# Two-layer diffusion trunk on one core: order of branch A's score matmuls, and two small PE jobs each placed one step later

## What is computed

```python
qa = qa.reshape(B, T, A_KV_HEADS, A_GROUP, HD)          # 2 key heads, 4 query heads each
s = jnp.einsum("bqhgd,bshd->bhgqs", qi, k) * scale
m = jnp.maximum(jnp.max(s, axis=-1, keepdims=True), sink)
e = jnp.exp(s - m)
p = e / (jnp.sum(e, axis=-1, keepdims=True) + jnp.exp(sink - m))
o = jnp.einsum("bhgqs,bshe->bqhge", p, v)
merged = ga * (oa @ w_branch_a) + gb * (od @ w_branch_b) + gc * (om @ w_branch_c)
```

## Time and profile before

| what | value |
|---|---|
| median of 3 runs | 1704.36 us (1704.34 to 1705.16) |
| the profiled execution, its own time | 1704.68 us |
| span from its first to its last instruction | 1702.9 us |
| mean granted TensorE clock, share of full speed | 0.997 |
| instructions in the trace | 21,074 |
| busy: PE, DVE, ACT, POOL | 98%, 25%, 19%, 7% of the span |
| moved by DMA | 561.94 MB, mean 330 GB/s |

### The profile page before, as it was taken

The page is one execution under the profiler, slowest core; times in us unless marked ns, Lnnn a source line. Parts: engine busy times, 40 slices in busy tenths (PEclk is TensorE's granted clock), DMA queues, the critical chain, the costliest instruction groups (busy, mean ns, idle before and its releaser), DMA issues. The chain is left out here.

```text
span 1702.9 us, 21074 instructions
## 1 busy us (share of the span) xinstructions
PE 1665.1 (98%) x8107; PEld 892.7 (52%) x8107; DVE 430.7 (25%) x1183; ACT 324.8 (19%) x786; POOL 120.0 (7%) x164
## 2 busy tenths in 40 slices
PE   5999999999999999999999999999999999999998
PEld 3778788543333333333368878884433333333332
DVE  1114444361111111111131444543411111111112
ACT  1010341121111111111120113403111111111111
POOL 3001000020000000001020000001100000000000
PEclk9999999999999999999999999999999999999999
DMA  9994233379999999999999732235899999999993
GB/s 388 397 410 164 76 117 118 118 282 419 425 426 424 425 425 426 425 425 424 420 389 422 292 115 99 99 110 207 323 426 425 426 425 425 426 425 424 426 425 159
DMA packets 61100, 561.94 MB, mean 330 GB/s; under 512 B 13020, under 2 KB 13168, under 8 KB 21072
## 3 DMA queue, kind: packets, MB, share of 16 engines
q1 hardware_dynamic: 45504, 529.55, 75.4%
q0 software_dynamic: 15504, 31.09, 5.3%
HBM read 575.95 MB, written 6.88 MB: 342 GB/s over the span
## 5 line engine op out<-in xcount | busy, mean ns | idle before, releaser
L1050 PE MATMUL PS<-ring,region 128*64 128x512 f32 x2048 | 451.0, 592 | 0.7 <-ACT region L1331 0.7
L1050 PEld LDWEIGHTS PS<-ring,region 128*64 128x64 f32 x2048 | 146.4, 137 | 290.4 <-issue 290.3
L617 PE MATMUL PS<-region,ring 128*128 128x256 f32 x1088 | 245.3, 381 | 0.5 <-DMA ring<-in_blocks 0.5
L1099 PE MATMUL PS<-region 128*128 128x512 f32 x512 | 241.0, 594 | 0.0
L1076 PE MATMUL PS<-ring,region 128*64 128x512 f32 x1024 | 233.8, 598 | 0.2
L617 PEld LDWEIGHTS PS<-region,ring 128*128 128x128 f32 x1088 | 203.8, 190 | 34.2 <-issue 6.3
L1804 DVE SCALAR_TENSOR_TENSOR region<-region,PS 128x256 f32<-128x256 f32 x64 | 26.9, 421 | 662.8 <-ACT region L1338 662.8
L510 PEld LDWEIGHTS PS<-const,region 128*128 128x128 f32 (+1 forms) x925 | 106.5, 141 | 115.7 <-issue 67.3
L510 PE MATMUL PS<-const,region 128*128 128x128 f32 (+1 forms) x925 | 137.8, 278 | 15.7 <-DMA region<-in_c 9.6
L1076 PEld LDWEIGHTS PS<-ring,region 128*64 128x64 f32 x1024 | 67.7, 136 | 157.4 <-issue 156.7
L1344 ACT ACTIVATE region<-PS 128x512 f32<-128x512 f32 x128 | 76.4, 597 | 265.9 <-PE PS L1076 265.9
(11 more groups left out here) (270 smaller groups left out, 991.2 us busy)
## 6 DMA issues: line engine op xcount, KB each, us to landing
ring<-in_expert_blocks SPq DMA_DIRECT2D x192, 2048.0 KB, 17.1
ring<-in_blocks SPq DMA_DIRECT2D x120, 1024.0 KB, 19.6
region<-post_rows POOLq DMA_DIRECT2D x8, 512.0 KB, 6.2
h_first<-region POOLq DMA_DIRECT2D x4, 512.0 KB, 6.4
h_table<-region POOLq DMA_DIRECT2D x4, 512.0 KB
region<-in_w_kvk POOLq DMA_DIRECT2D x2, 640.0 KB, 18.6
region<-in_mla_w_ukv POOLq DMA_DIRECT2D x2, 512.0 KB, 21.8
region<-in_post_pack POOLq DMA_DIRECT2D x2, 512.0 KB, 25.4
```

What stands on the lines that cost most here:

```text
L617: last = pe.matmul(PS[:, j % 2, m * T:(m + 1) * T], w[:, k, m * P:(m + 1) * P], hT[:, k, :], start=(k == 0), stop=(k == KC - 1))
L1050: last = pe.matmul(PS[e * CAP:(e + 1) * CAP, 0, :], xe[:, k, e * CAP:(e + 1) * CAP], w[:, k % 4, :], start=(k == 0), stop=(k == KC - 1), s ...
L1099: last = pe.matmul(PS[:, 4 + 2 * t + half, :], hot[:, t * P:(t + 1) * P], og[:, half * HALF:(half + 1) * HALF], start=False, stop=True, sk ...
```

## The change

Three edits, of which the second and third don't touch branch A.

- Scores of branch A: a unit now takes the same slots of both key heads in turn, each key head into a bank of its own (b and b + 1), so the heads of a unit are others than before: tile 0's unit g has slots 2g and 2g + 1 of both key heads, tile 1's unit g has slot g of both. The values, the place of the weight blocks, the exponentials' sources, the row maxima and the sink terms follow. The outputs stand in `qA` by slot, and the rows of `w_branch_a` are put in that order on the host. As two banks are written, the scores of units 0 and 1 wait for one more emptied job each.
- Counts: they come behind step 5 of the shared gate/up of tile 1 instead of behind step 4.
- List transposes: they come ahead of k = 3 of pair 0's gate/up instead of ahead of k = 2.

```diff
--- before.py
+++ after.py
@@ -779,16 +779,16 @@
                     q0, k0, kn = t * P, t * P, P + t * P
                     if u < 2:
 
-                        pe.wait_ge(prep_ev, l * PREP_JOBS + (21, 23)[u])
+                        pe.wait_ge(prep_ev, l * PREP_JOBS + (22, 24)[u])
                     else:
 
                         pe.wait_ge(prob_exp, (l * UNITS + u - 1) * 4)
                     n = 4 if t == 0 else 2
                     for i in range(n):
                         if br == "A":
-                            h = n * g + i
-                            kv, c = h // 4, h % 4
-                            last = pe.matmul(PS[:, b, i * kn:(i + 1) * kn], qA[HD * kv:HD * (kv + 1), c, q0:q0 + P],
+                            j, kv = divmod(i, 2)
+                            c = (n // 2) * g + j
+                            last = pe.matmul(PS[:, b + kv, j * kn:(j + 1) * kn], qA[HD * kv:HD * (kv + 1), c, q0:q0 + P],
                                              kA[HD * kv:HD * (kv + 1), k0:k0 + kn], start=True, stop=True)
                         elif br == "B":
 
@@ -825,7 +825,7 @@
                             h = heads * g + i
                             tile = kt + t
                             if br == "A":
-                                v = vA[:, tile, (h // 4) * HD:(h // 4 + 1) * HD]
+                                v = vA[:, tile, (i % 2) * HD:(i % 2 + 1) * HD]
                             elif br == "B":
                                 v = vB[:, tile, h * P:(h + 1) * P]
                             else:
@@ -834,7 +834,7 @@
                                 out = PS[:, 7, i * P:(i + 1) * P]
                             else:
                                 out = PS[HD * (i % 2):HD * (i % 2) + HD, 7, (i // 2) * P:(i // 2 + 1) * P]
-                            blk = i * (t + 1) + kt
+                            blk = (i % 2 * (heads // 2) + i // 2 if br == "A" else i) * (t + 1) + kt
                             weights = probT[:, u % 2, blk * P:(blk + 1) * P]
                             if br == "B":
                                 last = pe.matmul(out, weights, v, start=(kt == 0), stop=(kt == t), skip_group_check=True)
@@ -983,7 +983,7 @@
                 logits(1)
                 for half in range(2):
                     token_rows(1, half)
-                shared_gate_up(1, range(5))
+                shared_gate_up(1, range(6))
 
                 pe.wait_ge(sel_ready, l + 1)
                 pe.matmul(PS[:, 0, 0:N_EXPERTS], ones, sel[:, 0, :], start=True, stop=False)
@@ -995,7 +995,7 @@
                 for t in range(2):
                     last = transpose(PS[0:N_EXPERTS, 1, P + t * P:P + (t + 1) * P], sel[:, t, :])
                 last.then_inc(keys_tr, 1)
-                shared_gate_up(1, range(5, KC))
+                shared_gate_up(1, range(6, KC))
 
                 def first_tokens():
                     for t in range(2):
@@ -1044,7 +1044,7 @@
                                 n = 6 * g + 2 * (k // 4) + e
                                 if k % 4 == 0 and e == 0:
                                     arrived_pair(n, base)
-                                if g == 0 and k == 2 and e == 0:
+                                if g == 0 and k == 3 and e == 0:
                                     transpose_lists()
                                 w = ring[:, n % RING_SLOTS, :].rearrange("p (k c) -> p k c", k=4)
                                 last = pe.matmul(PS[e * CAP:(e + 1) * CAP, 0, :], xe[:, k, e * CAP:(e + 1) * CAP], w[:, k % 4, :],
@@ -1232,7 +1232,7 @@
                         act.activation(sinke[:, u % 2, 0:n], sinke[:, u % 2, 0:n], ACT.Exp).then_inc(sink_exp, 1)
                     for i in range(n):
                         m, j = divmod(i, n // 2)
-                        src = PS[:, b + m, j * kn:(j + 1) * kn] if br == "B" else PS[:, b, i * kn:(i + 1) * kn]
+                        src = PS[:, b + m, j * kn:(j + 1) * kn] if br in "AB" else PS[:, b, i * kn:(i + 1) * kn]
                         act.activation(prob[:, u % 2, i * kn:(i + 1) * kn], src, ACT.Exp,
                                        scale=(C_QK if br == "C" else HD) ** -0.5, bias=negm[:, u % 2, i:i + 1],
                                        accum_out=psums[:, u % 2, i:i + 1]).then_inc(prob_exp, 4 // n)
@@ -1606,16 +1606,17 @@
                     n, kn = (4, P) if t == 0 else (2, 2 * P)
                     scale = (C_QK if br == "C" else HD) ** -0.5
                     m = negm[:, u % 2, 0:n]
-                    if br == "B":
+                    if br in "AB":
                         s = PS[:, b:b + 2, 0:(n // 2) * kn].rearrange("p m (j k) -> p m j k", k=kn)
                         step(ve.reduce_max(m.rearrange("p (m j) -> p m j", m=2), s, X))
                     else:
                         step(ve.reduce_max(m, PS[:, b, :].rearrange("p (i k) -> p i k", k=kn), X))
                     if br == "A":
 
-                        ns = nsink[:, n * g:n * g + n]
+                        ns = nsink[:].rearrange("p (m c) -> p m c", m=2)[:, :, (n // 2) * g:(n // 2) * (g + 1)]
+                        m, e = (v.rearrange("p (m j) -> p m j", m=2) for v in (m, sinke[:, u % 2, 0:n]))
                         step(ve.scalar_tensor_tensor(out=m, in0=m, scalar=-scale, in1=ns, op0=ALU.mult, op1=ALU.min))
-                        ve.tensor_tensor(sinke[:, u % 2, 0:n], m, ns, ALU.subtract).then_inc(negm_ready, 1)
+                        ve.tensor_tensor(e, m, ns, ALU.subtract).then_inc(negm_ready, 1)
                     else:
                         ve.tensor_scalar(m, m, -scale, None, ALU.mult).then_inc(negm_ready, 1)
 
@@ -1874,9 +1875,10 @@
         put(L_UQ, w["mla_w_uq"][l])
         for j in range(10):
             put(L_GL + j, w_in[:, GL + 256 * (j + 2):GL + 256 * (j + 3)])
+        by_slots = w["w_branch_a"][l].reshape(A_KV, A_HEADS // A_KV, HD, -1).swapaxes(0, 1).reshape(A_HEADS * HD, -1)
         for half in range(2):
-            for b, name in enumerate(("w_branch_a", "w_branch_b", "w_branch_c")):
-                put(L_BR + 3 * half + b, w[name][l][:, 512 * half:512 * half + 512])
+            for b, matrix in enumerate((by_slots, w["w_branch_b"][l], w["w_branch_c"][l])):
+                put(L_BR + 3 * half + b, matrix[:, 512 * half:512 * half + 512])
         gate_up = np.concatenate([w["shared_w_gate"][l], w["shared_w_up"][l]], axis=1)
         for rows in range(2):
             for half in range(2):
```

## The result

The changed kernel takes **1712.31 us** (median, 1711.53 to 1713.75) against 1704.36 (1704.03 to 1705.16) for the kernel before: a ratio of 1.0043, with a 95% interval of 1.0032 to 1.0055. The median is higher by 8.0 us, clear of the noise, where no change was forecast, and it lies above the range. The profiled execution took 1713.43 us with a span of 1711.6 (before 1704.68 and 1702.9), so the two spans can be set beside each other: + 8.7 us.

The account below looks back on a forecast made before the run. The prediction took TensorE, busy for 98% of the span, as the bound. It summed - 5.1 us (scores) and + 4.6 us (later gather) to - 0.5 us, so 1703.9 us in the median's terms, no change, range 1697.6 to 1707.8.

Parts of the forecast that it names:

- Part 1: Branch A's scores: heads alternating halves and banks run at branch B's times, 5.1 us saved over both layers.
- The cover of 1.05 us: Branch A's unit step: 1.05 us spare between DVE's normalising and the weight transposes, so no new wait.
- Part 2: Counts one step later: wait before L989 gone, 0.45 us gained per layer, the rest a new wait before L1002.
- Part 3: List transposes one step later: L1032's wait gone, but pair 1's gather lands later, + 2.0 and + 2.6 us by layer.
- The line: Pair 1's gather time interpolated between leads of 1.32 and 0.01 us over the ring's load: 7.3 and 7.7 us.
- the 0.44 us of the prediction: Expected time from issue of pair 1's gather to issue of the ring's 2 MB load, 1.32 - 0.88 us.
- pair 2's gather: Gather issued 0.01 us ahead of the load, 8.7 and 9.2 us; used as the short-lead end of the interpolation.
- some 4 us: Expected PE wait on the table's rows for pair 1, in place of 0.6 and 0.85 us.
- Behind the load: Rival: pair 1's gather lands only with the ring's load, at 384.2 and 1220.5; 1707.8 us, chance 0.08.
- the rule of the Trainium skill: DMA engines take queues in turn, draining whole packets; read as the gather standing behind the load's share, not between its pieces.
- The gather isn't disturbed: Rival: pair 1's gather, still issued first, keeps its 4.32 and 4.56 us; - 6.6 us, 1697.8, chance 0.22.
- no overlap in part 1: Rival: branch A's halves don't overlap in the scores, so the 5.1 us falls away; 1709 us, chance 0.03.

Follow-up runs that it names:

- the run with the filled wait: Changed kernel plus seven unused 128x128 by 512 matmuls on PE between pair 0's gate/up and the wait for the gather; 1707.86 us, ratio 1.0018.
- a lead of 0.90: Kernel before plus sixteen tiny POOL memsets ahead of pair 1's gather, so the ring's load follows it by 0.90 and 0.93 us; 1709.46 us, ratio 1.0025.

## Why the prediction was wrong

**Part 1** held: 5.6 and 2.9 us by form and - 5.1 us measured alone. The cover of 1.05 us before the transposes was enough in branch A: the list of waits has 0.5 us on L1636 in two places, and the kernel before has the same 0.5 on L1635.

**Part 2** held by its own steps: L989 without a wait, a new wait before L1002 (0.25 us a layer where 0.4 was expected), and 0.6 us measured with an interval that can't confirm the size.

**Part 3** held as far as PE's waits go (none on L1032, none on L1813 behind the gathered rows). The prediction failed at one step of it: "Between leads of 1.32 and 0.01 us I go in a straight line". The line gave 7.3 and 7.7 us; measured were 9.9 and 10.0. That is 2.6 and 2.3 us too little even though the lead came out kinder than the 0.44 us of the prediction. The lead was 0.73, because DVE was free when the transposes came: from L1032 to POOL's issue took 372.07 - 370.44 = 1.63 us and not the 375.22 - 373.32 = 1.90 of the earlier trace rows. At 0.73 the line would have given 6.3. The table above shows no such line: the gather takes 3.9 to 5.3 us down to a lead of 1.2, 5.7 at 0.9, where the line's 5.7 and 6.0 happen to fit, and 9.8 and 9.3 at 0.76 and 0.78, where the line gives 6.2 and 6.6. The row it should have gone by was in front of me, pair 2's gather with 8.7 and 9.2 us: it was read as the far end of a slope, and it was the level that holds already at 0.78.

**What the sum lacked** is the clock. A wait of 6.8 us was in reach of the prediction (it expected "some 4 us" on the table's rows), and no term stood for what PE does after a wait. Some 4.5 us of the 8.0 are that, by the run with the filled wait. By its own steps: measured gather times in place of the line add 2.6 + 2.3 = 4.9 us. The issue came 0.2 us earlier in each layer (372.07 - 367.71 = 4.36 us after the start of gate/up, where the prediction had 375.05 - 370.51 = 4.54): - 0.4. The clock adds 4.5. So 1703.9 + 4.9 - 0.4 + 4.5 = 1712.9, against 1712.31. That it closes to 0.6 us is in part luck, as the clock's term is known to some 2.5 us only.

**The rivals.** *Behind the load* had the mechanism: the gather lands with the load. It put the landing 8.7 and 9.2 us after the load's issue; it was 381.95 - 372.80 = 9.15 and 1222.26 - 1213.02 = 9.24. It priced the wait right and had no clock either, which is why its 1707.8 falls short by about the same 4.5 us. The chance of 0.08 was too low, and for a wrong reason: "the gather has 0.44 us of lead". The prediction drew from the rule of the Trainium skill that the gather would stand behind the load's share and not between its pieces. The packets say that it does go between them, 76 beside 80, and lands with the load all the same; the lead of 0.44 us, or of 0.73, was no head start, since the gather's first row starts 1.7 us after its issue and the load's first packet 1.0 us after its own. *The gather isn't disturbed* and *no overlap in part 1* are both ruled out, the one by 9.9 us, the other by the forms of L791.

**What stays open.** In the changed kernel's first stretch the gather's 16 packets with a row take 0.60 us each on average, in the kernel before its 48 take 0.26, with q1 carrying as much in both (37 and 38 packets). The engines aren't full meanwhile: the two queues take 42.4 + 25.6 = 68% of them in the changed kernel and 90% in the kernel before. So it isn't for want of engine time, and why these packets are slower when both transfers start together no run here tells. Nor was a lead of 0.75 tried with the order of the kernel before, nor one between 0.78 and 0.90.

## What to carry to other kernels

Where a small transfer with someone waiting is issued just ahead of a big one, write down the lead and, from the trace, how long after its issue the first packet of each starts (here 1.7 and 1.0 us). If an edit brings the lead near the difference, 0.7 us here, price the small transfer at the big one's landing time and not between. A matmul moved past one queue's signal moves against every other signal of the same loop, and here moving the release along with it (k = 4 to 5) took the whole loss back. Put a term for the slow clock behind any new wait of TensorE: behind waits of 6.8 us it cost 2.2 us a layer on top, and waits of 1.7 and 2.5 us already brought it for a while.

## What was not expected of the hardware

- The step: gathers of one size take 3.9 to 5.3 us with a lead of 1.2 us or more over the load, 5.7 at 0.9, and 9.2 to 10.0 at 0.73 to 0.78, where the load's first packet starts together with the gather's first row.
- Near the step a kernel scatters: 8.0 us between seven executions at a lead of 0.90, against 2.2 between five of the changed kernel, which lies clearly behind it.
- The granted clock fell to 0.50 while PE was idle in a wait of 6.8 us, and stayed there through the first 6 us of work behind it. Idle time filled with useless matmuls is worth some 4.5 us here.
- Two POOL memsets of 128x8 take 0.14 us together and four 0.21, so each further one adds some 0.035 us: a row of small instructions is a poor delay line.
